# Output biases by the first turn's scatter, gate weights in two early slots, and the embedding gate's first steps by row block

## The chip, the cores and the metric

The kernel runs on one core of one Trainium2 chip, as one program with one launch. The metric is the device time of an execution in microseconds (us); less is better. PE is the matrix engine (TensorE), DVE the vector engine, ACT the scalar engine, POOL the GpSimd engine; SP only issues DMAs and waits. PSUM has eight banks of 128 partitions by 512 f32 words.

## The reference

Everything is f32, for 256 tokens of width 1024. A first block (pooling, attention, a mixture of experts, a gated embedding, a norm) is followed by two layers of another kind. What matters here is the end of the first block:

```
x = x + moe(rmsnorm(x, g_ffn), w_router, b_router, w_gate_up, b_gate_up, w_down, b_down)
gate = sigmoid(rmsnorm(x, g_ple) @ w_ple_gate)          # 1024 x 1024
x = x + (p @ w_ple_proj) * gate                         # p has 256 columns
x = rmsnorm(x, g_final)
```

In `moe` each token picks 4 of 32 experts; for a picked expert `e` with gate value `gate_e` it adds `gate_e * (act(h @ w_gate_up[e] + b_gate_up[e]) @ w_down[e] + b_down[e])`. So the output biases contribute, for each token, the sum over its experts of `gate_e * b_down[e]`. After the first block come two layers that begin with a feed-forward part: `x + 0.5 * swiglu(rmsnorm(x, ffa_norm), w_in, w_out)`.

## The kernel before

**Order.** Each engine has one hand-written list of instructions; engines wait for one another on semaphores only. Four pieces follow one another in each list: `first_part` (pooling and attention), `experts_part`, the gated embedding (the functions whose names begin with `ple_`), and two calls of the layer functions. SP's list sets the order of nearly all DMAs, on one queue.

**Experts.** The expert weights are 192 units of 2 MB (six to an expert), streamed through eight slots: `ring[0]` to `ring[5]`, and two in scratch (slots 6 and 7). The loop has one turn an expert for 64 tokens; `experts_part` first computes how many turns there are (`turns_ready`, here 32), and every engine loads that number into registers (`turns_of`) before its loop. In a turn PE multiplies the selected tokens `xsel` by units 0 to 3 (`product`, L2221), turns the result, gathers the next turn's tokens with a 0/1 matrix `sel` (`gather_turn`), turns `gsel` (the selection times the gates; `selT`), and multiplies by units 4 and 5 into the bank that ACT copies to `y`. The next turn's `scatter` (L2229, 4 matmuls with 64 rows each) adds `gselT` times `y` to four accumulators `acc(t, v)`: t is the block of 128 tokens, v the half of 512 columns. SP issues a unit's successor when PE has read it (L2135). Before turn 0 `y` and `gselT` are zero, so the first scatter adds nothing.

**Output biases.** They sit in scratch (`M_BDOWN`). After the loop PE turns `gate` (L2278), ACT copies it (L2323), PE adds the biases by 4 matmuls with only 32 rows (L2284), and then does the last scatter. The gate and up biases `b_gu` are loaded four times over, because the turn's number indexes them.

**Gated embedding.** SP loads `w_ple_proj` and the turned p into `ring[0]` after the last group's third turn (`ple_proj_sync`), and the two halves of `w_ple_gate` into scratch after the last unit is read (`ple_weights_sync`). PE: for each (t, v) two matmuls of p (`proj`, L2530) and four transposes of x (L2536); then four groups of eight matmuls (L2551), `pgate(v, t)`. DVE first sums all four accumulators into x (L2678), then scales the turned x (L2683). ACT: four squares, two roots, and then, in `ple_act`, `splits.to(SPLIT_SLOTS - 1)`, the casts of four pieces of the first layer's weights, and only then the first sigmoid:

```python
    splits.to(SPLIT_SLOTS - 1)
    for v in range(2):
        ple_sigmoid_act(k, act, 0, v)
        ple_squares_act(k, act, 0, v)
```

From there ACT and DVE alternate: sigmoid (L2566), product and sum (L2626 to L2628), squares (L2575, L2577), the variance (L2638 to L2647), a root, h (L2656); first for t = 0, v = 0 and 1, then for t = 1. PE turns h for the first layer (L750), between the two blocks it has 20 matmuls whose result nobody reads (`spare_pe`, L731), and then the feed-forward product starts (L831, L832).

**Layer weights.** SP sends the layers' weights in 0.5 MB pieces into four `raw` buffers (L2801). These lie over `ring[0]`, where the operands of `proj` are, so SP first waits:

```python
        k.enter("ple")
        k.filled(sp, ("proj", 1, 1))
        for layer in range(LAYERS):
```

ACT casts a piece to `w_hi` (L612), POOL computes the rest `w_lo` (L618).

Of the kernel before, what the change touches and what calls it, by code (L numbers as in the profile page):

```python
# [13 lines left out]
P = 128  # L14
# [263 lines left out]
def bc(ap, shape):  # L278
    return ap.to_broadcast(shape)
# [1482 lines left out]
def first_part(k, dram, block):  # L1762
# [11 lines left out]
    def _(sp):  # L1774
# [29 lines left out]

        sp.wait_ge(*k.at("rev_ready", 1))
# [209 lines left out]
SL = 64  # L2015
# [3 lines left out]
M_BGU, M_BDOWN, M_ROUTE = 5508, 7556, 8580  # L2019
# [42 lines left out]
def moe_uses(start):  # L2062
# [9 lines left out]
    uses.add(("gateT",), 0)  # L2072
# [6 lines left out]
def experts_part(k, dram, block):  # L2079
# [10 lines left out]
    def turn_filled(eng, key, it):  # L2090
        eng.wait_ge(full_of[key], it + (2 if key[0] == "gather" else 1))
        return k.bank[TURN_KEYS[key]], free_of[key]
# [6 lines left out]
    rank, gate, bgu = k.s(M_RANK, NT, TURNS), k.s(M_GATE, NT, TURNS), k.s(M_BGU, ROUNDS * E, 16)  # L2099
    b_down = k.s(M_BDOWN, D)  # L2100
# [4 lines left out]
    count, gateT, more = small(552, 1), small(560, NT, P), small(556, ROUNDS)  # L2105
# [12 lines left out]
    def _(sp):  # L2118
# [26 lines left out]
        sp.wait_ge(full_of["y",], last * GROUP + GROUP)  # L2145
        with k.inside("ple"):
            ple_weights_sync(k, sp, dram)
            ple_small_sync(k, sp, dram)

    @block.tensor  # L2150
    def _(pe):
# [11 lines left out]
        def gather(b, half, *rows_of):  # L2163

            for t in rows_of:
                for j in range(4):
                    c = 4 * half + j
                    last = nc.tensor.matmul(b[:, j * P:(j + 1) * P], k.h[:, t, c * P:(c + 1) * P], sel[:, t, :],
                                            start=(t + j == 0), stop=(t == 1 and j == 3))
            return last  # L2170
# [29 lines left out]
        k.evacuated(pe, ("count",), ("rank", 1))  # L2200
        turns, groups_n = turns_of(pe)
# [23 lines left out]
        def scatter(last=False):  # L2225
            for t in range(NT):
# [13 lines left out]
        with pe.Fori(0, groups_n) as group:  # L2240
            for turn in range(GROUP):
# [9 lines left out]
                scatter()  # L2251
# [13 lines left out]
                for t in range(NT):  # L2265
                    last = nc.tensor.transpose(b[:, t * P:(t + 1) * P], gsel[:, t, :], k.c("ident"))
                last.then_inc(full, 1)
# [5 lines left out]
        for half in range(2):  # L2273
            turn_evacuated(pe, ("gather", half), turns)
# [4 lines left out]
        last.then_inc(full, 1)  # L2279
        k.evacuated(pe, ("gateT",))  # L2280
        pe.wait_ge(*k.at("b_loaded", 16 * (ROUNDS + 1)))
        for t in range(NT):
            for v in range(2):
                nc.tensor.matmul(k.bank[4 + 2 * t + v][:, :], gateT[0:E, t, :], b_down[0:E, v * 512:(v + 1) * 512], start=False, stop=False)  # L2284
        for key in (("selT",), ("y",)):
            turn_evacuated(pe, key, turns)
        scatter(last=True)
        with k.inside("ple"):
            ple_first_pe(k, pe)

    @block.scalar
    def _(act):
# [14 lines left out]
        nc.scalar.activation(ex, ex, ACT.Exp).then_inc(k.sem("exp_ready"), 1)  # L2307
        turns, groups_n = turns_of(act)
# [13 lines left out]
        b, free = k.filled(act, ("gateT",))  # L2322
        nc.scalar.copy(gateT[0:E], part(b, NT, P)[0:E]).then_inc(free, 1)  # L2323

    @block.vector
    def _(dve):
# [57 lines left out]
        V_.memset(y, 0.0).then_inc(free_of["y",], 1)  # L2384
        V_.memset(gselT, 0.0).then_inc(free_of["selT",], 1)
        dve.wait_ge(free_of["y",], 1)
# [994 lines left out]
```

## Time and profile before

| what | value |
|---|---|
| median of 3 runs | 2469.76 us (2467.59 to 2471.13) |
| span of the profiled execution (first to last instruction) | 2465.0 us |
| the profiled execution's own time | not printed apart from its span; the runs are 2.6 to 6.1 us above the span |
| PE busy in the span | 2426.4 us (98%) |
| DVE, ACT, POOL busy | 924.0, 887.1, 1010.1 us |
| DMA in the expert loop | 430 GB/s |
| expert loop on PE | 119.95 us to about 1033.6 us |
| gated embedding on PE, up to the first product of layer 0 | about 1033.6 us to 1088.91 us |

Times in the rows are us from the span's start. A row of a chain of waits gives start, length, and what the end waited on. A row of a timeline gives start, length, engine, line, operation, tiles, shapes and count, with the idle time before it in brackets. A f32 matmul has two records.

### The profile page before, as it was taken

The page shows a single profiled execution, that of the slowest core. Times are in us where ns is not written, and L with a number is a line of the kernel's source. Part 1 is how long each engine was busy: PE and PEld are TensorE (multiplying, and loading weights), DVE is VectorE, ACT ScalarE, POOL GpSimd, SP SyncE. Part 2 cuts the span into 40 slices and gives each one's busy share as a digit, 9 for nine tenths or more (in the row PEclk, how much of TensorE's full clock was granted, in tenths as well). Part 3 has the DMA queues.
Part 4 walks back from the last instruction along what each step waited for, and adds up shares of the span by engine and source line. Part 5 has one row for each costly group of instructions (what it writes and reads, how often), then busy time and mean ns, then how long its engine had stood idle before and what let it go on. Part 6 is the DMA issues. An engine that isn't in the chain of part 4 may idle for free.

```text
span 2465.0 us, 34958 instructions
## 1 busy us (share of the span) xinstructions
PE 2426.4 (98%) x13879; PEld 1715.0 (70%) x13879; DVE 924.0 (37%) x1746; ACT 887.1 (36%) x1455; POOL 1010.1 (41%) x428
## 2 busy tenths in 40 slices
PE   8999999999999999999999999999999999999999
PEld 6744444444444444468889899888888898998887
DVE  5622222222222222253238764332432378653322
ACT  6411111111111111154457634544444477425443
POOL 0000000000000000038878445788788795546986
PEclk9999999999999999999999999999999999999999
DMA  7799999999999999935555333465555553324554
GB/s 285 292 399 428 430 430 429 430 429 430 430 429 430 429 430 430 381 120 199 189 168 178 105 103 129 155 209 189 177 189 193 169 175 120 120 95 154 200 185 144
DMA packets 96703, 653.66 MB, mean 265 GB/s; under 512 B 10880, under 2 KB 13232, under 8 KB 69968
## 3 DMA queue, kind: packets, MB, share of 16 engines
q1 hardware_dynamic: 96592, 652.11, 68.1%
q8 instruction: 78, 1.28, 0.2%
q14 instruction: 33, 0.27, 0.0%
HBM read 651.01 MB, written 1.06 MB: 265 GB/s over the span
## 4 chain that ended last, share of the span: by engine, by line
PE 87%; DMA 9%; DVE 1%; ACT 1%; issue 1%; POOL 0%; SPq 0%; DVEq 0%; ACTq 0%
PE bank L2221 20%; PE bank L831 13%; PE bank L631 10%; PE bank L633 10%; PE bank L632 10%; PE bank L832 7%; DMA ring<-in_expert_units 5%; DMA scratch<-in_expert_units 4%; PE bank L2208 4%; PE bank L1226 3%; PE bank L2229 2%; PE bank L2551 1%; PE bank L2237 1%; PE bank L1104 1%; PE bank L1075 1%
## 5 line engine op out<-in xcount | busy, mean ns | idle before, releaser
L618 POOL TENSOR_TENSOR w_lo<-raw,w_hi 128x1024 fp32r<-128x1024 f32 (+2 forms) x424 | 1009.9, 2410 | 1442.5 <-ACT w_hi L612 1442.5
L2221 PE MATMUL bank<-ring,scratch 128*64 128x512 f32 x2304 | 514.1, 596 | 12.8 <-DMA ring<-in_expert_units 11.7
L831 PE MATMUL bank<-hT_both,w_hi 128*128 128x512 f32 x1408 | 496.2, 398 | 1.7 <-DVE hT_both L722 1.7
L612 ACT CAST w_hi<-raw 128x1024 fp32r<-128x1024 f32 (+2 forms) x424 | 421.1, 1042 | 166.6 <-PE bank L633 159.2
L832 PE MATMUL bank<-hT_both,w_lo 128*128 128x256 f32 x1408 | 394.8, 280 | 0.0
L2221 PEld LDWEIGHTS bank<-ring,scratch 128*64 128x64 f32 x2304 | 160.5, 137 | 327.6 <-issue 321.7
L831 PEld LDWEIGHTS bank<-hT_both,w_hi 128*128 128x128 f32 x1408 | 264.7, 188 | 67.0 <-issue 3.0
L2461 DVE TENSOR_TENSOR scratch<-bank,scratch 128x512 f32<-128x512 f32 x64 | 44.3, 692 | 597.3 <-PE bank L2237 593.2
L832 PEld LDWEIGHTS bank<-hT_both,w_lo 128*128 128x128 f32 x1408 | 265.9, 189 | 0.6
L909 DVE TENSOR_REDUCE scratch<-bank 128x256 f32<-128x512 f32 x88 | 60.9, 692 | 356.6 <-PE bank L832 356.6
L2221 PE MATMUL bank<-scratch 128*64 128x512 f32 x768 | 172.1, 596 | 3.1 <-DMA scratch<-in_expert_units 3.1
L631 PE MATMUL bank<-hT_both,w_hi 128*128 128x256 f32 x576 | 165.6, 287 | 0.0
L633 PE MATMUL bank<-hT_both,w_lo 128*128 128x256 f32 x576 | 163.2, 283 | 0.0
L632 PE MATMUL bank<-hT_both,w_hi 128*128 128x256 f32 x576 | 163.1, 283 | 0.0
L631 PE MATMUL bank<-w_hi,act_hi 128*128 128x512 f32 (+1 forms) x376 | 145.9, 388 | 0.0
L632 PE MATMUL bank<-w_lo,act_hi 128*128 128x512 f32 (+1 forms) x376 | 145.8, 388 | 0.0
L633 PE MATMUL bank<-w_hi,act_lo 128*128 128x512 f32 (+1 forms) x376 | 145.7, 388 | 0.0
L2316 ACT ACTIVATE scratch<-scratch 128x256 f32<-128x256 f32 x64 | 26.7, 417 | 307.7 <-DVE scratch L2464 307.7
L2208 PEld LDWEIGHTS bank<-scratch,h_rows 128*128 128x128 f32 x1024 | 119.3, 192 | 26.0 <-issue 26.0
L2314 ACT COPY scratch<-bank 128x512 f32<-128x512 f32 x64 | 37.5, 585 | 269.3 <-PE bank L2221 269.3
L2221 PEld LDWEIGHTS bank<-scratch 128*64 128x64 f32 x768 | 53.5, 137 | 108.0 <-issue 106.9
L2208 PE MATMUL bank<-scratch,h_rows 128*128 128x128 f32 x1024 | 128.1, 278 | 0.0
(380 smaller groups left out, 3371.9 us busy)
## 6 DMA issues: line engine op xcount, KB each, us to landing
ring<-in_expert_units SPq DMA_DIRECT2D x144, 2048.0 KB, 29.6
raw<-in_layer_halves SPq DMA_DIRECT2D x408, 512.0 KB, 3.9
scratch<-in_expert_units SPq DMA_DIRECT2D x48, 2048.0 KB, 30.5
ring<-in_first_units SPq DMA_DIRECT2D x11, 1024.0 KB, 10.4
scratch<-in_ple_units SPq DMA_DIRECT2D x2, 2048.0 KB, 11.0
raw<-in_layer_halves SPq DMA_DIRECT2D x8, 424.0 KB, 3.2
scratch<-in_norm_gains SPq DMA_DIRECT2D x6, 512.0 KB, 5.8
raw<-in_layer_halves SPq DMA_DIRECT2D x4, 384.0 KB, 3.2
```

The lines of the kernel that those rows point to most:

```text
L612: k.nc.scalar.copy(k.w[0][i % SPLIT_SLOTS][:, at], k.raw[n % RAW_SLOTS][:, 0:at.stop - at.start]).then_inc(k.shared("weights_hi"), 1)
L618: k.nc.gpsimd.tensor_tensor(k.w[1][i % SPLIT_SLOTS][:, at], k.raw[n % RAW_SLOTS][:, 0:at.stop - at.start], k.w[0][i % SPLIT_SLOTS][:, at], ...
L631: nc.tensor.matmul(out, lhsT[0], rhs[0], start=start, stop=False)
L632: nc.tensor.matmul(out, lhsT[0], rhs[1], start=False, stop=False)
L633: return nc.tensor.matmul(out, lhsT[1], rhs[0], start=False, stop=stop)
L831: nc.tensor.matmul(bank[:, :], w[0], both, start=start, stop=False)
L832: return nc.tensor.matmul(bank[:, 0:S], w[1], both[:, 0:S], start=False, stop=stop)
L909: return k.nc.vector.tensor_reduce(out, b[:, :].rearrange("p (part n) -> p n part", part=2), AX.X, ALU.add)
L1226: last = nc.tensor.matmul(b[:, h * P:(h + 1) * P], lhsT[:, h, :], rhs[:, h, :], start=True, stop=True)
L2208: last = nc.tensor.matmul(b[:, j * P:(j + 1) * P], k.h[:, t, c * P:(c + 1) * P], sel[:, t, :], start=(t == 0), stop=(t == 1))
L2221: last = nc.tensor.matmul(b[g * SL:(g + 1) * SL, :], lhsT[:, c, :], w[:, c, g, :], start=start and c == 0, stop=stop and c == 3)
L2229: ins = nc.tensor.matmul(k.bank[b][:, :], gselT[half, t, :], y[half, :], start=False, stop=last)
```

## The change

The output biases are loaded near the kernel's start into rows 0 to 31 (columns 0 to 511) and 64 to 95 (columns 512 to 1023) of `y`, which DVE has zeroed. Before the loop DVE writes the gates of all experts into `gsel` in the same two places, PE turns them, ACT copies them to `gselT`, and turn 0's scatter, which used to add zeros, adds the biases. The block behind the loop (turn, copy, 4 matmuls) is gone. `b_gu` is loaded once, indexed by the turn's number modulo 32. The gate's denominators are computed before the count of turns instead of after the first `take`.

The halves of `w_ple_gate` go to `ring[4]` and `ring[5]`, each as soon as the last expert has read that slot. PE's list behind the loop is now: proj(0,0), last scatter, proj(0,1), transposes of t = 0, proj(1,0), gate products (0, v = 0), transposes of t = 1, gate products (0, v = 1), proj(1,1), and the two gate products of t = 1. In this sentence proj(t, v) has the block first. DVE sums and scales one block, then the other.

```diff
@@ first_part, SP, behind load(7)
+        sp.wait_ge(*k.at("zeros_ready", 1))
+        with k.inside("moe"):
+            moe_down_biases_sync(k, sp, dram)
         sp.wait_ge(*k.at("rev_ready", 1))
@@ first_part, DVE
+        nc.vector.memset(k.s(M_Y, 512), 0.0)
         link(nc.vector.memset(k.hT[:, 0:2, :], 0.0))
@@
 def moe_biases_sync(k, sp, dram):
-    bgu, b_down = k.s(M_BGU, ROUNDS * E, 16), k.s(M_BDOWN, D)
-    for r in range(ROUNDS):
-        sp.dma_start(bgu[:, r * E:(r + 1) * E, :], dram["b_gu"]).then_inc(k.sem("b_loaded"), 16)
-    sp.dma_start(b_down[0:E, :], dram["b_down"].rearrange("o e d -> (o e) d")).then_inc(k.sem("b_loaded"), 16)
+    sp.dma_start(k.s(M_BGU, E, 16), dram["b_gu"]).then_inc(k.sem("b_loaded"), 16)
+
+def moe_down_biases_sync(k, sp, dram):
+    y, b_down = k.s(M_Y, 512), dram["b_down"].rearrange("o e d -> (o e) d")
+    for v in range(2):
+        sp.dma_start(y[v * SL:v * SL + E, :], b_down[:, columns_half(v)]).then_inc(k.sem("b_loaded"), 16)
@@ experts_part, SP
-        sp.wait_ge(full_of["y",], last * GROUP + GROUP)
+        sp.wait_ge(k.sem("first_unit_read"), last * (GROUP * EXPERT_UNITS // 2) + (GROUP - 1) * EXPERT_UNITS // 2 + 2)
         with k.inside("ple"):
-            ple_weights_sync(k, sp, dram)
+            ple_weights_sync(k, sp, dram, 0)
+        sp.wait_ge(full_of["rows", 1], last * GROUP + GROUP)
+        with k.inside("ple"):
+            ple_weights_sync(k, sp, dram, 1)
             ple_small_sync(k, sp, dram)
@@ experts_part, PE, ahead of the loop
         k.evacuated(pe, ("count",), ("rank", 1))
+        pe.wait_ge(*k.at("gate_ready", 1))
+        selection_turned(k.bank[TURN_KEYS["selT",]]).then_inc(full_of["selT",], 1)
         turns, groups_n = turns_of(pe)
@@ experts_part, PE, behind the loop
-        b, full = k.claim(pe, ("gateT",))
-        pe.wait_ge(*k.at("gate_ready", 1))
         for t in range(NT):
-            last = nc.tensor.transpose(b[0:E, t * P:(t + 1) * P], gate[:, t, 0:E], k.c("ident"))
-        last.then_inc(full, 1)
-        k.evacuated(pe, ("gateT",))
-        pe.wait_ge(*k.at("b_loaded", 16 * (ROUNDS + 1)))
-        for t in range(NT):
-            for v in range(2):
-                nc.tensor.matmul(k.bank[4 + 2 * t + v][:, :], gateT[0:E, t, :], b_down[0:E, v * 512:(v + 1) * 512], start=False, stop=False)
-        for key in (("selT",), ("y",)):
-            turn_evacuated(pe, key, turns)
-        scatter(last=True)
+            scatter((t,), last=True)
         with k.inside("ple"):
-            ple_first_pe(k, pe)
+            ple_proj_pe(k, pe, 0, 1)
+            ple_turned_pe(k, pe, 0)
+            ple_proj_pe(k, pe, 1, 0)
...
@@ experts_part, DVE, between sel_ready and the count of turns
+        dve.wait_ge(*k.at("exp_ready", 1))
+        link(V_.tensor_tensor(ex, ex, chosen, ALU.mult))
+        link(V_.tensor_reduce(den, ex, AX.X, ALU.add))
+        link(V_.reciprocal(den, den))
+        for t in range(NT):
+            ins = V_.tensor_scalar(gsel[:, t, :].rearrange("p (v n) -> p v n", v=2)[:, :, 0:E], bc(ex[:, t, :].unsqueeze(1), [P, 2, E]),
+                                   den[:, t:t + 1], None, ALU.mult)
+        ins.then_inc(k.sem("gate_ready"), 1)
+
         b, free = k.filled(dve, ("count",))
@@ layers_part, PE
-        ple_gate_pe(k, pe)
+        ple_gate_pe(k, pe, 0, 0)
+        ple_turned_pe(k, pe, 1)
+        ple_gate_pe(k, pe, 0, 1)
+        ple_proj_pe(k, pe, 1, 1)
+        ple_gate_pe(k, pe, 1, 0)
+        ple_gate_pe(k, pe, 1, 1)
```

Nothing in `ple_act`, in SP's wait for `proj(1,1)`, or in the layers is changed.

## Rows read from the trace of the kernel before

**Rows 1.** Page, part 4: the chain that ended last, share by engine.

```profile
PE 87%; DMA 9%; DVE 1%; ACT 1%; issue 1%; POOL 0%; SPq 0%; DVEq 0%; ACTq 0%
```

**Rows 2.** The chain from 1015 to 1130 us: start, length, what.

```profile
1026.64 7.04 PE bank L2221 x32
...
1034.59 5.45 PE bank L2284 x8
1040.04 3.51 PE bank L2229 x8
...
1045.46 0.44 PE bank L2536 x4
1045.90 1.72 PE bank L2530 x4
...
1052.37 27.48 PE bank L2551 x64
```

**Rows 3.** The chain of the whole span: turn 0's scatter.

```profile
127.04 1.92 PE bank L2229 x8
```

**Rows 4.** Stretches of 1 us: length, busy PE, PEld, DVE, ACT, POOL, clock, DMA, GB/s.

```profile
1036.00:1037.00 1.00, 1.00 (x3) 0.51 (x2) 0.00 (x0) 0.00 (x0) 0.00 (x0) 0.70 0.81 344
...
1043.00:1044.00 1.00, 1.00 (x3) 0.30 (x2) 0.78 (x2) 1.00 (x4) 0.00 (x0) 0.89 1.07 459
```

**Rows 5.** Timeline from the layer weights' first DMA to the first sigmoid.

```profile
1051.96 67.61 SPq L2801 DMA_DIRECT2D raw<-in_layer_halves  x18
...
1055.91 1.05 ACT L612 CAST w_hi<-raw 128x1024 fp32r<-128x1024 f32 x1 [1.69 <-DMA raw<-in_layer_halves]
...
1060.33 1.04 ACT L612 CAST w_hi<-raw 128x1024 fp32r<-128x1024 f32 x1 [0.21 <-DMA raw<-in_layer_halves]
...
1062.69 0.69 ACT L2566 ACTIVATE scratch<-bank,scratch 128x512 f32<-128x512 f32 x1
```

**Rows 6.** Timelines of DVE, ACT and PE, from h to the feed-forward product.

```profile
1072.71 1.41 DVE L2656 SCALAR_TENSOR_TENSOR h_rows<-bank,scratch 128x512 f32<-128x512 f32 x2 [0.49 <-ACT scratch L2585]
...
1085.89 1.41 DVE L2656 SCALAR_TENSOR_TENSOR h_rows<-bank,scratch 128x512 f32<-128x512 f32 x2 [0.27 <-ACT scratch L2585]
...
1079.94 0.69 ACT L2566 ACTIVATE scratch<-bank,scratch 128x512 f32<-128x512 f32 x1 [1.10 <-PE bank L2551]
...
1080.47 4.81 PE L731 MATMUL bank<-w_hi 128*128 128x512 f32 x20
...
1088.91 0.47 PE L831 MATMUL bank<-hT_both,w_hi 128*128 128x512 f32 x1 [0.90 <-DVE hT_both L722]
```

**Rows 7.** Timeline ahead of the expert loop: end of the count, gates, first product.

```profile
117.80 0.14 DVE L2429 CAST scratch<-scratch 128x1 int32<-128x1 f32 x1
...
119.26 0.22 DVE L2438 TENSOR_TENSOR scratch<-scratch 128x64 f32<-128x64 f32 x1
...
119.95 7.09 PE L2221 MATMUL bank<-ring,scratch 128*64 128x512 f32 x32 [1.07 <-issue]
119.96 0.63 DVE L2442 TENSOR_TENSOR scratch<-scratch 128x64 f32<-128x64 f32 x4
```

**Rows 8.** Stretches in the expert loop, columns as in rows 4.

```profile
124.00:125.00 1.00, 1.00 (x8) 0.31 (x5) 0.00 (x0) 0.00 (x0) 0.00 (x0) 1.00 0.04 16
...
145.00:146.00 1.00, 1.00 (x8) 0.41 (x6) 0.00 (x0) 0.00 (x0) 0.00 (x0) 1.00 0.31 131
...
300.00:600.00 300.00, 300.00 (x1574) 129.50 (x1574) 68.37 (x176) 39.69 (x71) 0.00 (x0) 1.00 1.01 430
```

**Rows 9.** Timeline of the kernel's first microseconds.

```profile
0.92 0.48 DVE L1973 MEMSET hT<- 128x512 f32 x1 [0.92 <-PEq L3377]
...
1.92 3.78 PE L512 MATMUL bank<-first_lo 128*128 128x512 f32 x8 [1.92 <-DVE first_lo L1974]
```

**Rows 10.** SP's timeline, then the page's DMA issues: KB, median us to landing.

```profile
1004.42 0.34 SPq L2504 DMA_DIRECT2D ring<-in_ple_units  x1
...
ring<-in_ple_units SPq DMA_DIRECT2D x1, 1024.0 KB, 26.3
```

More of the change, by code:

```diff
@@ L2104, in experts_part @@
     den = small(550, NT)
[L2105 removed]
+    count, more = small(552, 1), small(556, ROUNDS)
     turns_i, groups_i, groups = small(553, 1).bitcast(I32), small(554, 1).bitcast(I32), small(555, 1)
@@ L2223, in product, with scatter @@
             return last
-        def scatter(last=False):
-            for t in range(NT):
+        def scatter(rows_of, last=False):
+            for t in rows_of:
                 for v in range(2):
@@ L2264, in _ @@
                 b, full = turn_claim(pe, ("selT",), it)
-                for t in range(NT):
-                    last = nc.tensor.transpose(b[:, t * P:(t + 1) * P], gsel[:, t, :], k.c("ident"))
-                last.then_inc(full, 1)
+                selection_turned(b).then_inc(full, 1)
                 b, full = turn_claim(pe, ("y",), it)
@@ L2307, in _ @@
         nc.scalar.activation(ex, ex, ACT.Exp).then_inc(k.sem("exp_ready"), 1)
+        act.wait_ge(full_of["selT",], 1)
+        nc.scalar.copy(gselT, part(k.bank[TURN_KEYS["selT",]], NT, P)).then_inc(free_of["selT",], 1)
         turns, groups_n = turns_of(act)
@@ L2395, in _ @@
         h_of(0)
+        dve.wait_ge(*k.at("b_loaded", 3 * 16))
+        V_.memset(gsel, 0.0).then_inc(free_of["y",], 1)
         hT_of(1, 0)
@@ L2540, in ple_gate_pe @@
-def ple_gate_pe(k, pe):
-    hT = k.s(PLE_HT, KC, S)
-    for t in range(NT):
-        for v in range(2):
-            if t == 0:
-                pe.wait_ge(*k.at(f"ple_arrived{v}", 16))
-            w = k.s(PLE_W[v], KC, 512)
-            k.evacuated(pe, ("norm", 0, t, 0), ("norm", 0, t, 1))
-            b, full = k.claim(pe, ("pgate", v, t))
-            for c in range(KC):
-                last = k.nc.tensor.matmul(b[:, :], hT[:, c, t * P:(t + 1) * P], w[:, c, :], start=(c == 0), stop=(c == KC - 1))
-            last.then_inc(full, 1)
+    b, full = k.claim(pe, ("proj", v, t))
@@ new lines, in ple_proj_pe, with ple_turned_pe, ple_gate_pe @@
+    for c in range(2):
+        last = k.nc.tensor.matmul(b[:, :], pT[:, c, t * P:(t + 1) * P], w[:, c, v * 512:(v + 1) * 512], start=(c == 0), stop=(c == 1))
+    last.then_inc(full, 1)
+def ple_turned_pe(k, pe, t):
+    for v in range(2):
+        b, full = k.claim(pe, ("norm", 0, t, v))
+        for j in range(4):
+            c = 4 * v + j
+            last = k.nc.tensor.transpose(b[:, j * P:(j + 1) * P], k.x[:, t, c * P:(c + 1) * P], k.c("ident"))
+        last.then_inc(full, 1)
+def ple_gate_pe(k, pe, t, v):
+    hT, w = k.s(PLE_HT, KC, S), ple_gate_weights(k, v).rearrange("p (c n) -> p c n", n=512)
+    if t == 0:
+        pe.wait_ge(*k.at(f"ple_arrived{v}", 16))
+    for c in range(KC):
+        if c % 4 == 0:
+            k.evacuated(pe, ("norm", 0, t, c // 4))
+            if c == 0:
+                b, full = k.claim(pe, ("pgate", v, t))
+        last = k.nc.tensor.matmul(b[:, :], hT[:, c, t * P:(t + 1) * P], w[:, c, :], start=(c == 0), stop=(c == KC - 1))
+    last.then_inc(full, 1)
```

71 lines of the change are left out of this document (26 added, 45 removed).

## The prediction, made before the changed kernel was run

> **What bounds the kernel now.** I read the page's chain first, then the chain of waits by stretch, then the timelines at the three places the change touches. PE carries 87% of the chain that ended last [rows 1], so time is won only where PE's list gets shorter and nothing else ends later. There are three regimes. Inside the expert loop PE is at first the slower one; DMA runs dry twice, at 124 us and again at 145 us, because a unit's successor can only be sent when PE has read its slot, and from then on it moves 430 GB/s without a pause to the end of the loop [rows 8]. So the loop ends a fixed time after PE begins it, and bytes taken out before it are worth nothing: all eight slots are full when DMA stops at 124. Behind the loop, PE is busy from 1033.68 us (1026.64 + 7.04) through the bias products, the scatter, the p products and the 64 gate records to about 1079.85 [rows 2]. The reader should then see how thin PE's lead is: ACT's last sigmoid waited only 1.10 us for PE [rows 6]. Just behind PE runs a second chain: SP sends layer weights at 1051.96, when the last proj product is done; ACT casts four pieces (first at 1055.91, the fourth ends 1060.33 + 1.04 = 1061.37), loads its table, and starts the first sigmoid at 1062.69 [rows 5]. From there ACT and DVE alternate without a pause that PE causes, up to that 1.10 us.
>
> **PE's list behind the loop.** Before: 1033.68 to 1079.85 is 46.2 us. Removed: the turn, ACT's copy and the four 32-row matmuls, from 1033.68 to 1040.04, 6.4 us [rows 2]. The scatter took 3.51 us there and 1.92 in the loop [rows 2, 3], the same eight records. The granted clock explains it: it left full speed (2.4 GHz) at about 1036.3 us (mean 0.70 in 1036 to 1037) and came back at about 1043.1 (0.89 in 1043 to 1044) [rows 4], and what PE did before was the pause for ACT's copy and then the 32-row matmuls. Without them I expect full speed, so 1.92. New list: 4 proj groups at 1.72, 4 transpose groups at 0.44, the scatter at 1.92, 64 gate records at 27.48 / 64 = 0.43: 6.88 + 1.76 + 1.92 + 27.48 = 38.0 us [rows 2, 3]. PE saves 8.1 us. What hides the waits: proj(0,0) (1.72) covers ACT's copy of y, a single copy of one bank, shorter than that; scatter(1) and proj(0,1) (2.7 us) cover DVE's two sums of block 0, and proj(1,0) with the second transposes its two scalings. Each of these four handles one bank of 512 columns, about half of L2656's 1.41 us for two [rows 6]; without that cover each would show once, 0.7 us. The sums of block 1 have the 6.9 us of the first gate group.
>
> **The weights.** proj's operands are issued at 1004.42 and land 26.3 us later, 1030.7 [rows 10], 3 us ahead of their use now at 1033.7. `w_ple_gate` is sent some 11 to 15 us earlier than before, behind those on the same queue. At 430 GB/s [rows 8] a half takes 4.9 us, so they land at about 1036 and 1041; PE wants them at about 1042 and 1050. No expert unit waits behind them. Worth 0; before, they were no wait either.
>
> **Where the stall goes.** SP's wait for proj(1,1) is untouched, since `raw` lies over `ring[0]`. But proj(1,1) now comes behind two groups of gate products. Between the end of the loop and it PE has 4 x 1.72 + 1.92 + 4 x 0.44 + 32 records x 0.43 (13.74) = 24.3 us; before it was 1051.96 - 1033.68 = 18.3 [rows 2, 3, 5]. The first layer piece leaves 6.0 us later, relative to the end of the loop. Queued behind it: the landing (3.95 us to the first cast), four casts on ACT, which stand ahead of the first sigmoid in ACT's list, and the table load; 10.73 us from the DMA to the sigmoid, as before [rows 5]. DVE waits for the sigmoids, and PE for DVE's h. So the whole ACT and DVE chain moves 6.0 us later, though the first gate bank was full 10 us before. It gets back only the 1.10 us that the last sigmoid had waited for PE [rows 6]. Net on the path: 6.0 - 1.1 = +4.9 us where PE alone would say -8.1. DVE's and ACT's own work is the same, and the layer behind is PE's, so nothing later takes it back. POOL's four pieces also end 6 us later, before `spare_pe` needs them.
>
> **Before the loop.** Turn 0's scatter does what it did, with other numbers. On DVE five instructions now stand ahead of the count of turns. Three of them took 119.26 to 119.96, 0.70 us; two writes of `gsel` at 0.63 / 4 = 0.16 each make 1.0 us [rows 7]. The count ended at 117.80 + 0.14, and PE's first product came 2.0 us later, with 1.07 us of pause that nothing explains but the loading of registers; PE's gathers were done before. So the loop starts up to 1.0 us late. Below: if PE's pause hangs on its gathers alone, 0.4 us, for two more transposes (a group of four is 0.44 [rows 2]). I take 1.0, because DVE shows the same two microseconds between the end of its gates, 120.59, and its first loop work. What stood there for 0.6 to 0.7 us leaves a place where DVE is not late. The new memset of `y` stands ahead of everything on DVE. The memset of `hT` took 0.48 us, and PE's first matmul waited for its cast until 1.92 [rows 9]; its warming matmuls run until x is turned. So +0.5, between 0 (if x had not arrived) and 0.5. The two new bias loads are issued while SP would wait for the distance table: 0, and if that cover were gone, two issues at 0.34 us [rows 10]. The saved loads of `b_gu`: 0, by the idle DMA at 124 us [rows 8]. `it & 31` costs DVE a register step in a loop where it idles: 0. The front together: +1.5.
>
> **The clock.** PE is done at 1033.7 + 1.5 + 38.0 = 1073.2, and h of block 0 comes at 1072.71 + 7.5 = 1080.2 [rows 6]: 7 us or more in which PE has nothing. `spare_pe` (4.81 us) follows, and then PE waits again, from about 1086 to h of block 1 at 1085.89 + 6.4 = 1092.3 [rows 6]. Before, no pause was near this long, and the one fall of the clock lasted 6.8 us [rows 4]. What falls before spare work costs nothing. What is still low when the feed-forward product begins costs half of its time: between 0 and 3.4 us (half of 6.8). I take the middle, +1.7, as neither row is near.
>
> Against this stands a rule of the Trainium skill, page "TensorE: Matmul & The Clock Gate", section "Why this matters for your kernels": pauses between bursts of matmuls put the clock back to its lower level. By it both pauses end at 1.2 GHz. That is rival 1.
>
> **Sum.** -1.1 + 6.0 + 1.5 + 1.7 = +8.1 us. The profiled execution's span would go from 2465.0 to 2473.1. The median of the runs is 4.8 us above the span before, and I carry the difference: 2469.8 + 8.1 = 2477.9. The feed-forward product L831 begins at 1088.91 + 6.4 = 1095.3.
>
> **Rivals.**
> 1. The clock's fall in full: low for 6.8 us from the start of the feed-forward product. 4.9 + 1.5 + 3.4 = +9.8, 2479.6. For it: two pauses of 6 to 8 us, where a short one and narrow matmuls were enough. Against: `spare_pe` between them.
> 2. Clock and front are both free: only the late weights, +4.9, 2474.7. For it: PE paused 1.07 us ahead of the loop already [rows 7], so a part of a delay there may be absorbed. Against: the register loads on DVE and PE follow the count.
> 3. The other side, faster: the place is ACT's list between the fourth cast and the first sigmoid. If the pieces don't hold the sigmoids, because they land and are cast while PE works on the second gate group, PE's end decides: -8.1 + 1.5 = -6.6, 2463.2. It decides if the fourth cast ends no later than before plus 1.1 us relative to the sigmoid chain, that is if the piece leaves no more than 1.1 us later. Against: SP's wait is on proj(1,1), two gate groups down PE's list, and ACT works in order. The rows leave little room.
>
> **Chances.** Forecast 0.60, rival 1 0.17, rival 2 0.15, rival 3 0.08. What a measurement of this kernel can tell from no change is 0.2%, 4.9 us: below 2464.8 faster, above 2474.7 slower. Rival 2 sits on that border, so half of it, and a little of the forecast's lower end, is "same": 0.09. Slower 0.83, faster 0.08. Range 2472.5 to 2483: the chain term alone less a miscount of a group, up to rival 1 with the runs' own spread (1.8 us) on top. It leaves out rival 3 and a tail.
>
> **What the profile after would show.** Behind the loop no L2278, L2284, L2323, the last scatter at 1.9 us and the clock at 1.00 through it; proj(1,1) and SP's first raw piece at about 1059.5; the first sigmoid at about 1070.2, right behind the fourth cast; PE idle from about 1073 to 1081 and again before 1092; L831 first at about 1095.3, and the clock there below 1.00. The first expert product at about 121.5. The prediction is wrong if the first sigmoid comes before 1064, if the raw pieces leave before proj(1,1), or if PE has work up to h of block 0.

## The result, and the profile after

The changed kernel takes 2479.36 us (median of 4 runs, 2477.68 to 2482.16), the kernel before 2468.68 (4 runs, 2464.10 to 2471.13): ratio 1.0047, 95% interval 1.0035 to 1.0058, so slower by 11.6 us (the two medians differ by 10.7). The forecast was 2477.9 and slower. The profiled execution took 2479.33 us with a span of 2477.5 us, 12.5 more than the span before. Lines moved down by 14 to 18: L2229 is L2246, L2530 L2544, L2536 L2554, L2551 L2568, L2566 L2583, L2656 L2673, L2801 L2817. L612, L731, L750 and L831 are unchanged.

PE's list behind the loop is what the forecast made of it: 38.4 us from the end of the loop to the end of the gate groups, where 38.0 was forecast. The chain of waits of the changed kernel from 1015 to 1130 us (start, length, what), which answers to [rows 2]:

```profile
1035.14 1.91 PE bank L2544 x4
1037.05 1.92 PE bank L2246 x8
1038.97 1.91 PE bank L2544 x4
1040.88 0.87 PE bank L2554 x8
1041.76 1.72 PE bank L2544 x4
1043.47 6.87 PE bank L2568 x16
1050.34 0.87 PE bank L2554 x8
1051.21 6.87 PE bank L2568 x16
1058.08 1.73 PE bank L2544 x4
...
1061.15 7.10 DMA raw<-in_layer_halves
...
1070.63 0.69 ACT scratch L2583
```

The bias products and the turning of `gate` are gone, and the scatter takes 1.92 us where it took 3.51. But the chain leaves PE at 1059.81, the end of p product (1,1). From there it is a DMA, ACT and DVE. PE's own third and fourth gate groups don't stand in it. The timelines of SP and ACT, for [rows 5]:

```profile
1059.83 12.47 SPq L2817 DMA_DIRECT2D raw<-in_layer_halves  x7
```

```profile
1063.84 1.05 ACT L612 CAST w_hi<-raw 128x1024 fp32r<-128x1024 f32 x1 [10.61 <-DMA raw<-in_layer_halves]
...
1068.28 1.04 ACT L612 CAST w_hi<-raw 128x1024 fp32r<-128x1024 f32 x1 [0.20 <-DMA raw<-in_layer_halves]
...
1070.63 0.69 ACT L2583 ACTIVATE scratch<-bank,scratch 128x512 f32<-128x512 f32 x1
...
1081.94 0.69 ACT L2583 ACTIVATE scratch<-bank,scratch 128x512 f32<-128x512 f32 x1
```

ACT sat idle for 10.61 us before its first cast, although the first gate bank was full at 1050.34. The last two sigmoids wait for no PE now, where the last one waited 1.10 us [rows 6]. What PE has left is two pauses. Its timeline from 1080 us on:

```profile
1081.46 1.97 PE L750 MATMUL bank<-const,h_rows 128*128 128x128 f32 x8 [7.93 <-DVE h_rows L2673]
1083.08 5.58 PE L731 MATMUL bank<-w_hi 128*128 128x512 f32 x20
1093.43 1.97 PE L750 MATMUL bank<-const,h_rows 128*128 128x128 f32 x8 [4.76 <-DVE h_rows L2673]
1096.10 0.77 PE L831 MATMUL bank<-hT_both,w_hi 128*128 128x512 f32 x1 [0.71 <-DVE hT_both L722]
```

The clock stands in the seventh place after the time in the stretches (columns as in rows 4). It stayed full through the scatter, and was at its lower level, 1.2 GHz, from 1077.9 to 1084.7 and from 1091.6 to 1101.8, 5.7 us of that inside the feed-forward product:

```profile
1036.00:1037.00 1.00, 1.00 (x5) 0.21 (x3) 0.00 (x0) 0.00 (x0) 0.00 (x0) 1.00 1.00 426
...
1092.00:1094.00 2.00, 0.57 (x3) 0.58 (x4) 1.69 (x4) 0.20 (x1) 0.00 (x0) 0.50 0.00 0
1096.00:1097.00 1.00, 0.90 (x3) 0.83 (x4) 0.88 (x2) 1.00 (x3) 0.00 (x0) 0.50 0.00 0
1101.00:1102.00 1.00, 1.00 (x5) 0.81 (x5) 1.00 (x4) 0.00 (x0) 0.78 (x1) 0.60 1.01 360
```

The front, for [rows 7, 9]. Two memsets now stand ahead of the cast, and the gates (from 117.27) ahead of the count:

```profile
0.92 0.48 DVE L1976 MEMSET scratch<- 128x512 f32 x1 [0.92 <-PEq L3398]
...
2.46 0.79 PE L512 MATMUL bank<-first_lo 128*128 128x512 f32 x1 [2.46 <-DVE first_lo L1978]
```

```profile
117.27 0.22 DVE L2428 TENSOR_TENSOR scratch<-scratch 128x64 f32<-128x64 f32 x1
...
119.42 0.14 DVE L2448 CAST scratch<-scratch 128x1 int32<-128x1 f32 x1
...
121.41 1.94 PE L2238 MATMUL bank<-ring,scratch 128*64 128x512 f32 x8 [1.73 <-issue]
```

The same instructions of both traces, set side by side, give the shift of after against before: 0.54 us at PE's first product, 1.46 at the first expert product, 1.46 at the end of the loop, 7.87 at the first raw piece, 7.94 at the first sigmoid, 6.73 at the transposes of block 1, 7.19 at L831, 9.75 at 1108 us (times of such a comparison are those of the first profile of before). Behind that it is still 9.8 at 1550 us, grows in two steps to 11.4 at 1850, and is 12.5 at the end of the span.

### The profile page after: what moved, and what is told of

It is laid out like the page before. It is cut to its first block, busy times and chain, and to the rows that moved or that the text cites. A ratio compares the mean times of both kernels' runs of the same rounds, so it can differ in the third digit from the quotient of the medians.

```text
span 2477.5 us, 34979 instructions
## 1 busy us (share of the span) xinstructions
PE 2426.1 (98%) x13871; PEld 1717.1 (69%) x13871; DVE 922.9 (37%) x1748; ACT 888.0 (36%) x1455; POOL 1009.6 (41%) x428
## 3 DMA queue, kind: packets, MB, share of 16 engines
q8 instruction: 78, 1.28, 0.2%
## 4 chain that ended last, share of the span: by engine, by line
PE 86%; DMA 10%; DVE 2%; ACT 1%; issue 1%; POOL 0%; SPq 0%; DVEq 0%; ACTq 0%
PE bank L2238 20%; PE bank L831 13%; PE bank L631 10%; PE bank L632 10%; PE bank L633 10%; PE bank L832 7%; DMA ring<-in_expert_units 5%; DMA scratch<-in_expert_units 4%; PE bank L2225 4%; PE bank L1226 3%; PE bank L2246 2%; PE bank L2254 1%; PE bank L1104 1%; PE bank L1075 1%; PE bank L2568 1%
## 5 line engine op out<-in xcount | busy, mean ns | idle before, releaser
L831 PE MATMUL bank<-hT_both,w_hi 128*128 128x512 f32 x1408 | 500.2, 400 | 1.5 <-DVE hT_both L722 1.5
L612 ACT CAST w_hi<-raw 128x1024 fp32r<-128x1024 f32 (+2 forms) x424 | 421.9, 1042 | 179.7 <-PE bank L633 157.9
L832 PE MATMUL bank<-hT_both,w_lo 128*128 128x256 f32 x1408 | 396.4, 282 | 0.0
L831 PEld LDWEIGHTS bank<-hT_both,w_hi 128*128 128x128 f32 x1408 | 265.7, 189 | 68.5 <-issue 3.2
L832 PEld LDWEIGHTS bank<-hT_both,w_lo 128*128 128x128 f32 x1408 | 267.2, 190 | 0.6
```

Of the source, the lines that this page charges most:

```text
L612: k.nc.scalar.copy(k.w[0][i % SPLIT_SLOTS][:, at], k.raw[n % RAW_SLOTS][:, 0:at.stop - at.start]).then_inc(k.shared("weights_hi"), 1)
L831: nc.tensor.matmul(bank[:, :], w[0], both, start=start, stop=False)
L832: return nc.tensor.matmul(bank[:, 0:S], w[1], both[:, 0:S], start=False, stop=stop)
```

## The experiments

My theory is the forecast's: p product (1,1) comes late, SP holds the raw pieces for it, and ACT's four casts of them stand ahead of every sigmoid. What else could make the same time is PE's own order, the clock, the front, and the weights or biases in their new places. Each verdict is read against the kernel before, run on the same chip. The medians of two kernels that did not run together compare less well: where a sentence below subtracts such medians, the ratios in the table say how much of it is safe.

| kernel | median us (runs) | before, same chip | ratio, 95% interval |
|---|---|---|---|
| changed kernel | 2479.36 (4) | 2468.68 | 1.0047 [1.0035, 1.0058] |
| e1_proj_early | 2466.89 (11) | 2468.11 | 0.9996 [0.9987, 1.0005] |
| e2_casts_behind | 2464.47 (11) | 2468.11 | 0.9984 [0.9975, 0.9993] |
| e4_clock_kept | 2483.99 (5) | 2468.11 | 1.0064 [1.0050, 1.0077] |
| e7_early_front | 2465.87 (11) | 2468.11 | 0.9991 [0.9982, 1.0000] |
| e5_blocks_undone | 2463.97 (11) | 2467.97 | 0.9984 [0.9975, 0.9992] |
| e6_late_weights | 2466.15 (11) | 2467.97 | 0.9995 [0.9987, 1.0004] |
| e8_casts_between | 2462.85 (12) | 2467.97 | 0.9987 [0.9978, 0.9995] |
| e9_clock_second | 2476.22 (5) | 2467.97 | 1.0033 [1.0020, 1.0046] |
| e3_front | 2476.27 (6) | 2467.39 | 1.0043 [1.0030, 1.0056] |
| e10_undone_front | 2461.84 (10) | 2467.39 | 0.9976 [0.9967, 0.9985] |
| e11_before_again | 2473.06 (1) | 2467.39 | one run |

**e1_proj_early.** One call moved in PE's list.

```diff
+        ple_proj_pe(k, pe, 1, 1)
         ple_gate_pe(k, pe, 0, 0)
         ple_turned_pe(k, pe, 1)
         ple_gate_pe(k, pe, 0, 1)
-        ple_proj_pe(k, pe, 1, 1)
         ple_gate_pe(k, pe, 1, 0)
```

> The changed kernel with one line of PE's list moved: proj(1,1) stands ahead of the first gate group instead of behind the second. Theory (the layer weights leave late, and ACT's casts of them hold the sigmoids): the first raw piece leaves at about 1045.2 us instead of 1059.8, the first sigmoid starts at about 1058.8 instead of 1070.6 (now it waits for the roots and four casts), PE has no pause before h of block 0, the clock stays up, and the first L831 comes at about 1083.9 instead of 1096.1. Span about 2462.4 (2477.5 - 12.2 - 3 for the clock), so some 6 us under the kernel before. Rival (the new order by blocks, or the work ahead of the loop, is what costs, and the weights only happen to leave later): first L831 stays at 1094 or later and the span at 2474 or more. Rival (only the clock's fall in the pauses costs): about 2474.

All of the loss is gone, by moving two matmuls (four records); the kernel takes the same time as before within the noise. SP sends the first piece at 1045.48 us, and ACT's timeline no longer shows a wait for a DMA. The pieces lie ready when the roots are done. SP's line and ACT's:

```profile
1045.48 1.85 SPq L2817 DMA_DIRECT2D raw<-in_layer_halves  x4
```

```profile
1055.12 3.87 ACT L612 CAST w_hi<-raw 128x1024 fp32r<-128x1024 f32 x4
...
1060.30 0.69 ACT L2583 ACTIVATE scratch<-bank,scratch 128x512 f32<-128x512 f32 x1
```

The casts themselves now hold the sigmoid for their 3.87 us. L831 begins at 1085.77, 3.1 us ahead of before. Here the expectation missed: it had 1083.9 with the clock up. PE idled 3.87 us before block 1's transposes, the clock was at its lower level from 1082.0 to 1088.8, and by 1099 the lead was 1.76 us. The span, 2465.2, is 2.8 above the one expected.

**e2_casts_behind.** The other end of the same wait: PE keeps the changed order, ACT casts after block 0's root.

```diff
-    splits.to(SPLIT_SLOTS - 1)
     for v in range(2):
         ple_sigmoid_act(k, act, 0, v)
         ple_squares_act(k, act, 0, v)
     with k.inside(0):
         ple_root_act(k, act, 0)
+    splits.to(SPLIT_SLOTS - 1)
```

> The changed kernel with PE's list as it is, and one line of ACT's list moved: the casts of the first four layer pieces stand behind block 0's root instead of ahead of the first sigmoid. Theory: the raw pieces still leave at about 1059.8, but the first sigmoid starts at about 1054.5 and the sigmoid of block 1 follows the casts at about 1070.6; PE has no pause before h of block 0; first L831 at about 1083.8, span about 2462.3. If what matters is when the pieces leave, and not ACT's order (a rival: the layer itself waits for its weights), L831 stays near 1094 to 1096 although the sigmoids come early.

This separates PE's order from the casts. The raw pieces leave as late as in the changed kernel (1063.13, in an execution that was 4.8 us late against before at the first expert product, where the changed kernel's was 1.46; its clock was low from 11.9 to 15.3 and again from 18.8 to 22.2 us), and 14.9 us of time are gone all the same. Less the 3.3 us between these two, the first sigmoid (1057.85) and L831 (1087.23) are within 0.2 us of what was expected. PE's order by row block costs next to nothing by itself; it costs through what ACT does in order. ACT's timeline:

```profile
1057.85 0.69 ACT L2583 ACTIVATE scratch<-bank,scratch 128x512 f32<-128x512 f32 x1
...
1067.75 1.98 ACT L612 CAST w_hi<-raw 128x1024 fp32r<-128x1024 f32 x2
```

**e4_clock_kept.** Spare matmuls in both pauses: 28 ahead of block 0's transposes, 44 behind.

```diff
+    if k.part == 0:
+        spare_pe(k, pe, 28)
     lnorm_pe(k, pe, 0, 0)
     if k.part == 0:
-        spare_pe(k, pe)
+        spare_pe(k, pe, 44)
```

> The changed kernel with more matmuls whose result nobody reads in PE's two pauses: 28 ahead of the transposes of h of block 0, 44 instead of 20 behind them. They keep PE busy and wait for nothing on the path. Theory: the granted clock stays at 1.00 at the start of the feed-forward product, the first L831 comes at about 1095.7 (1096.1 less the slow transposes), the product's first 6 us lose nothing, and the span is about 3 us less, 2474.5. Rival (the clock is not what costs between 1096 and 1108; the late layer weights are): the clock stays up and the span doesn't change, 2477. Rival (the clock is the whole loss): about 2465.

It misfired as a repair. The spare work borrows a bank that ACT's third sigmoid frees, so it could not start in the pause. PE's timeline:

```profile
1082.04 9.49 PE L731 MATMUL bank<-w_hi 128*128 128x512 f32 x28 [8.78 <-ACT scratch L2583]
...
1092.16 10.25 PE L731 MATMUL bank<-w_hi 128*128 128x512 f32 x44
...
1104.41 0.47 PE L831 MATMUL bank<-hT_both,w_hi 128*128 128x512 f32 x1 [1.12 <-DVE hT_both L722]
```

The fillers pushed L831 8.3 us later than in the changed kernel, and the time grew by only 4.6 (medians of kernels that did not run together): from L831 on the clock was full, and the shift against before did not grow (15.5 us there, 15.6 at 1500 us). The span is 7.3 us above the expected 2474.5, so this run says what a full clock does behind L831 and nothing about a repair.

**e9_clock_second.** The repair of that test: only the second pause is filled.

```diff
-    for j in range(20):
+    for j in range(40):
...
-                           start=(j == 0), stop=(j == 19))
+                           start=(j == 0), stop=(j == 39))
```

> The changed kernel with 40 spare matmuls instead of 20 between the two row blocks' transposes, so that TensorE works from 1083.1 to about 1093.3, where it was idle from 1088.7 to 1093.4. The first fall of the clock (1077.9 to 1084.7) stays. Theory (the second fall costs the transposes and the first feed-forward product about 3 us): clock at 1.00 from about 1085 on, the four last transposes take 0.7 instead of 1.13 us, the first feed-forward product starts at 1095.0 to 1095.8 instead of 1096.1, the shift against the kernel before stays at about 6.5 through 1108 instead of growing to 9.75, time 2475 to 2477. Rival (the extra shift behind the first product has another cause, weights arriving late for one): time 2479 to 2480 although the clock stays up.

PE worked until 0.46 us before the transposes, which took 1.32 us together instead of 1.97. PE's timeline and a stretch:

```profile
1084.72 9.88 PE L731 MATMUL bank<-w_hi 128*128 128x512 f32 x40
1095.06 1.32 PE L750 MATMUL bank<-const,h_rows 128*128 128x128 f32 x8 [0.46 <-DVE h_rows L2673]
1097.28 0.47 PE L831 MATMUL bank<-hT_both,w_hi 128*128 128x512 f32 x1 [0.90 <-DVE hT_both L722]
```

```profile
1096.00:1098.00 2.00, 1.10 (x8) 0.80 (x7) 1.56 (x3) 1.93 (x4) 0.00 (x0) 1.00 0.00 0
```

The start times are 1.7 us above what was expected, because this execution was already 3.12 us late at the first expert product, where the changed kernel's was 1.46. From there to 1096 us it lost 5.1 us against before (3.12 to 8.24), where the changed kernel lost 8.3 (1.46 to 9.74). The median is 3.1 us lower. Both say that the second fall costs about 3 us.

**e7_early_front** and **e3_front.** One edit on the front, on e1 and on the changed kernel: the new memset behind the cast, the gates and their transposes behind the count.

```diff
-        nc.vector.memset(k.s(M_Y, 512), 0.0)
         link(nc.vector.memset(k.hT[:, 0:2, :], 0.0))
...
+        nc.vector.memset(k.s(M_Y, 512), 0.0).then_inc(k.sem("y_cleared"), 1)
...
-        pe.wait_ge(*k.at("gate_ready", 1))
-        selection_turned(k.bank[TURN_KEYS["selT",]]).then_inc(full_of["selT",], 1)
         turns, groups_n = turns_of(pe)
+        pe.wait_ge(*k.at("gate_ready", 1))
+        selection_turned(k.bank[TURN_KEYS["selT",]]).then_inc(full_of["selT",], 1)
```

> proj(1,1) early as in the first of these, and the work ahead of the loop moved too: the new memset stands behind the cast that PE's first matmul waits for, the gates and their writes stand behind the count of turns on DVE, and PE turns them after it has loaded its registers. Theory: PE's first matmul starts 0.54 us earlier, the first expert product at about 120.2 instead of 121.4, and all behind moves with it: 1.2 us less than with proj(1,1) early alone, span about 2461.2. Rival (the loop ends when DMA has moved its bytes, and where PE begins it is worth nothing): the loop's end doesn't move, and the span is that of the kernel with proj(1,1) early.

> The changed kernel with its front put back in order: the first memset stands behind the cast of zeros, and the gates (VectorE) and their transposes (TensorE) stand behind the count of the turns. Theory (0.5 us for the memset ahead of the first product and 1.0 us for the gates ahead of the count, both carried to the end): first product at 1.9 instead of 2.46, first expert product at 120.0 to 120.4 instead of 121.4 where the clock at the start is the same, time 1.0 to 1.8 us below the changed kernel's 2479.4: 2477.6 to 2478.4. Rival (the loop takes the late start back while it waits for weights): the loop ends where it did, time 2479 to 2480.

In e7 the first expert product comes at 120.11 us, 1.62 ahead of e1, and the end of the loop and L831 both come 1.28 ahead (L831 at 1084.49): the loop does not take the start back. Its span, 2463.4, is 2.2 above the one expected, as e1's was 2.8 above its own.

In e3 PE's first product stands at 1.92 us again and the first expert product at 119.73, 1.68 earlier than in the changed kernel. All of that arrives at block 1's transposes, at 5.05 us of shift instead of 6.73. The line of its PE timeline:

```profile
119.73 1.51 PE L2238 MATMUL bank<-ring,scratch 128*64 128x512 f32 x6
```

By medians the repair gives 1.0 us in e7, 2.1 in e10 (below) and 3.1 in e3. The last two compare kernels that did not run together, and against before the ratios of e3 and the changed kernel differ by 0.0004, 1 us. e3's median, 2476.27, lies 1.3 us below the range expected for it. Its trace shows one reason: the second fall of the clock lasted 6.8 us (1090.4 to 1097.3) where the changed kernel's lasted 10.2, which is some 1.3 of the 3.1 us between the two traces at 1096. A stretch of e3 and then of the changed kernel:

```profile
1098.00:1100.00 2.00, 2.00 (x14) 1.75 (x13) 2.00 (x1) 0.00 (x0) 2.00 (x1) 1.00 0.54 160
```

```profile
1098.00:1100.00 2.00, 2.00 (x8) 1.71 (x7) 2.00 (x4) 1.21 (x1) 2.00 (x2) 0.50 0.00 0
```

So the front is worth 1 to 2 us.

**e5_blocks_undone.** The part with the block order undone, everything else of the change kept.

```diff
+        scatter(range(NT), last=True)
+        with k.inside("ple"):
+            for t in range(NT):
+                for v in range(2):
+                    ple_proj_pe(k, pe, t, v)
+                    ple_turned_pe(k, pe, t, (v,))
...
+        for t in range(NT):
+            for v in range(2):
+                ple_gate_pe(k, pe, t, v)
```

> The changed kernel with one part undone: TensorE issues the p products, the transposes of x and the gate groups in the order of the kernel before (all four scatters, then p product and transpose by half, then four gate groups), and VectorE makes all four x sums first. The biases in the first scatter, the weights in slots 4 and 5 and the new front stay. Theory (the row-block order lets go of the raw pieces late, and that is what the time went to): the loop still ends at about 1035.1, the raw pieces go out at about 1045.7 instead of 1059.8, the first sigmoid starts at 1058 to 1061, the first feed-forward product at 1083 to 1086, and the time is 2466 to 2470. Rival (the biases or the weights in ring slots cost it): the time stays at 2476 to 2481.

4.0 us faster than before, 15.4 below the changed kernel. So the order by row block, with ACT's list as it is, costs 15 us, and the rest of the change is a gain. Some 3 us of that (2466.89 against 2463.97) stay when only p product (1,1) is moved, as in e1: there ACT's last root stands at 1055.01, here at 1049.88 although this execution reached the loop 1.5 us later, and the sigmoids follow. The time is 2 us below the range expected. The end of the loop (1036.64) and the first raw piece (1047.82) came 1.5 and 2.1 us later than expected, as this execution was 3.3 us late at the first expert product instead of 1.5 (the clock had fallen once more in its first 15 us); the first sigmoid and L831 fell into their ranges. PE's and ACT's timelines:

```profile
1048.06 27.63 PE L2567 MATMUL bank<-ring,scratch 128*128 128x512 f32 x64
...
1076.32 4.81 PE L731 MATMUL bank<-w_hi 128*128 128x512 f32 x20
1082.55 1.31 PE L750 MATMUL bank<-const,h_rows 128*128 128x128 f32 x8 [1.42 <-DVE h_rows L2672]
1084.77 0.47 PE L831 MATMUL bank<-hT_both,w_hi 128*128 128x512 f32 x1 [0.90 <-DVE hT_both L722]
```

```profile
1051.83 1.04 ACT L612 CAST w_hi<-raw 128x1024 fp32r<-128x1024 f32 x1 [1.75 <-DMA raw<-in_layer_halves]
...
1058.68 0.69 ACT L2582 ACTIVATE scratch<-bank,scratch 128x512 f32<-128x512 f32 x1
```

**e6_late_weights.** As e5, with the gate weights sent after the last unit is read.

```diff
-        sp.wait_ge(k.sem("first_unit_read"), last * (GROUP * EXPERT_UNITS // 2) + (GROUP - 1) * EXPERT_UNITS // 2 + 2)
+        sp.wait_ge(full_of["y",], last * GROUP + GROUP)
         with k.inside("ple"):
             ple_weights_sync(k, sp, dram, 0)
-        sp.wait_ge(full_of["rows", 1], last * GROUP + GROUP)
-        with k.inside("ple"):
             ple_weights_sync(k, sp, dram, 1)
```

> As the run with the block order undone, and the gate weights are sent only when the last unit has been read (about 1035), into the same slots 4 and 5. Theory (early weights buy nothing while the first gate group starts at about 1046): they land at 1043 to 1047, the first gate group starts 0 to 1 us later than with early weights, and the time is within 1.5 us of that run. Rival (early weights are what keeps TensorE fed): the gate groups start 4 us or more later and the time grows by 4 us.

Neither theory as written. PE's gate groups start in their place (1048.42, no wait), and yet the time is 2.2 us above e5's. The price stands on ACT: the raw pieces, sent 0.35 us later than in e5, queue behind the weights and the small loads. The first sigmoid comes 3.0 us after e5's, PE pauses 2.98 us before block 1's transposes instead of 1.42, and in this execution the clock is low from 1083.7 to 1090.5, which it never is there in e5. So by the traces the 2.2 us are the late pieces and a fall of the clock together. ACT's timeline and a stretch, whose last two columns say that the DMA engines were busy all of it, at 383 GB/s:

```profile
1055.57 1.04 ACT L612 CAST w_hi<-raw 128x1024 fp32r<-128x1024 f32 x1 [5.13 <-DMA raw<-in_layer_halves]
```

```profile
1050.00:1054.00 4.00, 4.00 (x11) 1.71 (x9) 0.78 (x3) 0.20 (x1) 0.00 (x0) 1.00 1.01 383
```

**e8_casts_between.** e7, and the four casts go two by two into ACT's waits for DVE.

```diff
-    splits.to(SPLIT_SLOTS - 1)
     for v in range(2):
         ple_sigmoid_act(k, act, 0, v)
+        splits.to(SPLIT_SLOTS - 2 + v)
         ple_squares_act(k, act, 0, v)
```

> The version with p product (1,1) ahead of the first gate group and with the gates behind the count (2465.9), and ScalarE's four casts of raw pieces, 3.87 us that stood ahead of the first sigmoid at 1059.0, go two by two into its waits between sigmoid and squares of row block 0 (2.33 us each). Theory (ScalarE's list in front of the sigmoids sets the end, not TensorE's gate groups): first sigmoid at about 1055, root of row block 0 at about 1065, first feed-forward product at 1080.5 to 1082 instead of 1084.5, TensorE's pause before the last transposes 1 to 2 us instead of 3.9, so that the clock may stay at 1.00; time 2460 to 2463. Rival (the gate groups, which end at 1072.5, or GpSimd's low halves set the end): first product at 1084 to 1085, time 2465 to 2467.

As expected, but for the clock, which may have stayed up and did not. ACT's timeline shows two casts taking 1.98 us of a wait of 2.3, with 0.45 left:

```profile
1055.00 0.69 ACT L2583 ACTIVATE scratch<-bank,scratch 128x512 f32<-128x512 f32 x1
1055.59 1.98 ACT L612 CAST w_hi<-raw 128x1024 fp32r<-128x1024 f32 x2
1058.01 0.60 ACT L2592 ACTIVATE scratch<-bank 128x512 f32<-128x512 f32 x1 [0.45 <-DVE h_rows L2645]
```

L831 begins at 1081.65, 2.8 us ahead of e7's 1084.49. The clock still fell, from 1081.1 to 1084.5, after a pause of 1.72 us. The times don't separate the two kernels clearly: the medians differ by 3.0 us, but they did not run together, and the ratios against before differ by 0.0004, 1 us.

**e10_undone_front.** e5 with the front of e3.

> The version with the block order undone (2463.97) and the same repair of the front: what is left of the change is the biases in the first scatter and the weights in slots 4 and 5. Theory: 1.0 to 1.8 us below that version, 2462.2 to 2463.0, and below the kernel before by 5 to 6 us. Rival (its front costs nothing there): 2463.5 to 2464.5.

2461.84 us, the lowest median of this study, 0.4 us below the range expected: 5.6 us, 0.24% below before (0.15 to 0.33%). The intervals of e2, e5 and e8 overlap this one. What it keeps is the biases in the first scatter and the early weights. In its profiled execution L831 began at 1081.82, 7.1 us ahead of before, and the clock never fell after 5.8 us.

**e11_before_again.** The kernel before, profiled once more.

> The kernel before, profiled a second time. The changed kernel's profiled execution is 12.5 us longer in span than the one of before, but the medians differ by 9.6 to 11.6 us, and some 2.8 us of the 12.5 appear little by little in the two layers. Theory (the first profiled execution of before was one of its short ones, 2465.0 us against a median of 2468 to 2470): this one has a span of 2465.5 to 2469, and the shift against the first creeps up by 1 to 3 us behind the first feed-forward product as well. Rival (the changed kernel loses 2.8 us in the layers): no such creep, span 2464.5 to 2465.5.

Its span was 2471.2, longer than expected. The shift against the first profile is 1.9 us at the first expert product, 2.7 at the end of the loop, 1.0 at block 1's transposes and at L831, 3.8 at 1096 us and 6.2 at the end. So 2.4 us appear behind 1096 in the same kernel. The step of 2.8 before that is the clock, low from 1089.3 to 1096.1. So is the gain of 1.7 between the loop and the transposes: behind the loop the clock was low for 3.4 us here (1041.5 to 1044.9) and for 6.8 in the first profile, and the bias matmuls took 3.7 us instead of 5.45. Stretches of the second and then of the first profile of before:

```profile
1088.00:1090.00 2.00, 1.09 (x9) 0.65 (x7) 1.22 (x3) 1.50 (x3) 0.00 (x0) 0.82 0.00 0
1090.00:1092.00 2.00, 2.00 (x6) 1.71 (x7) 2.00 (x4) 1.98 (x3) 1.31 (x1) 0.50 0.03 8
```

```profile
1090.00:1092.00 2.00, 2.00 (x13) 1.76 (x12) 2.00 (x4) 1.81 (x2) 2.00 (x1) 1.00 0.04 8
```

## Why the prediction was right, and which terms were off

| term | predicted | measured | from |
|---|---|---|---|
| front | +1.5 | +1.46 | 0.54 at the first product, 0.92 more at the first expert product |
| late raw pieces | +6.0 | +6.4 | 7.87 - 1.46 |
| wait for PE given back | -1.1 | -1.2 | 7.94 at the first sigmoid, 6.73 at block 1's transposes |
| clock | +1.7 | +3.0 | 0.46 in the transposes, 2.56 from L831 to 1108 us |
| sum | +8.1 | +9.75 | shift at 1108 us (the rows above give 9.66) |
| layers | 0 | +2.8 | shift at the end 12.5 |

**The chain.** The mechanism held at each link: proj(1,1), SP, landing, casts, sigmoids. e1 cuts the first link and e2 the one between the casts and the sigmoids; each alone removes the whole loss (e1 the same as before, e2 0.16% below it). The gap of 0.4 us is a count made with 1.72 for each p product, where two of the four took 1.91.

**PE's list.** PE's gate groups ended at 1079.85 before and at 1073.53 after (1081.46 - 7.93): 6.3 us earlier, where 8.1 - 1.5 = 6.6 was forecast. Where the block order and with it the wait for raw pieces is undone and the front repaired (e10), L831 comes 7.1 us earlier and the time is 5.6 lower. That is the forecast's rival 3, which had -6.6 with the front still late. Its mechanism is real; its condition, that the pieces leave no more than 1.1 us later, was missed by 5.3 us. The gain was turned into a pause of PE. Some of the 8.1 us is the execution's: the list that the change removes and shortens took 46.2 us in the first profile of before and 44.5 in e11, as the clock was low for less of it.

**Front.** Right in both parts, and e3 confirms it. The loop passed the delay on undiminished (1.46 at its start and at its end), so rival 2, which had the front free, falls.

**Clock.** This is the mis-sized term. I took the middle of 0 and 3.4; the second fall cost 3.0, since it lasted 10.2 us, not 6.8, and 5.7 of these fell into the feed-forward product. In e3's execution, with two pauses much like them (7.60 and 4.49 us), it lasted 6.8 and cost about 1.6 (0.46 in the transposes, 1.17 from L831 to 1096), which is the forecast's figure; so the size of this term was not in the kernel alone. Rival 1's time, 2479.6, is nearer to the result than the forecast's, and what I held against it, `spare_pe` between the pauses, did not help: the spare work ended 4.8 us before block 1's h. The rule of the Trainium skill (page "TensorE: Matmul & The Clock Gate", section "Why this matters for your kernels") holds: both pauses ended at 1.2 GHz. e9 prices the second at about 3 us by filling it. But the reference was off too. The profile of before that I worked from shows no fall there, and e11 shows one that costs 2.8 us for the same code and the same pause (1.40 us). So the kernel before pays this in some of its executions, and the change's share of the clock, in the median, probably lies below 3.0; how often before pays was not measured.

**Layers.** The forecast had nothing there. Of the 2.8 us, 1.6 are two steps, at 1580 to 1650 and 1780 to 1850 us. They are a matter of the execution: e11 has both and a third at 2280 to 2350 (2.4 together) in the kernel before, and e3, with the changed kernel's layers, has none. The other 1.2 stand behind VectorE's last instruction, where the span goes on for 2.4 us in both profiles of before, 2.9 in e3 and six others, and 3.6 in the changed kernel, e2, e5 and e7; at most 0.5 of that is common to all the changed kernels. e11 also says what the 4.8 us were that I carried from span to median. Of them 1.8 are time outside the span (2479.33 - 2477.5, and 2473.06 - 2471.2 in e11). The other 3.0 made up for a short profiled execution. So it is partly luck that 2477.9 is only 1.5 us off: the span that was forecast, 2473.1, is 4.4 us short of the measured 2477.5, and 3.0 came back through the carried difference. Where the steps come from was not tried.

**Weights.** "Worth 0" holds for this kernel, where the pieces leave at 1059.8, long after the weights have landed. In e5's order it is worth 2.2 us (e5 and e6 ran together), not by PE but by the pieces behind them on the queue; the forecast had looked only at who reads the weights.

## What to carry to other kernels

Before an instruction is moved down one engine's list, look up who waits for its semaphore beyond the data it makes: here two matmuls that take 1.7 us together freed a buffer, and the DMA into it stood ahead of ACT's whole remaining list. A shorter list on the busiest engine shows in the time only if nothing in order on a second engine is made to wait for its later items; where the second engine has a wait of fixed length anyway (2.3 us here), put the work that nobody needs yet into it. And profile the kernel before twice: on one chip its executions ran from 2463.16 to 2472.43 us, nearly as far apart as the change is from it, and 2.8 us of the 6.2 between its two profiles are one fall of the clock.

## What was not expected of the hardware

The same pause gave two clocks. In two executions of the kernel before, with 1.42 and 1.40 us idle ahead of the last transposes, the clock stayed at 1.00 in the first and was at 0.50 from 1089.3 to 1096.1 in the second; e5 and e10 kept it after 1.42 us, e8 lost it for 3.4 us after 1.72 and e2 for 3.4 after 1.96. And the start varies: in five of the thirteen profiles (e2, e5, e6, e9, e11) the clock fell to 0.50 once more, from about 10.7 to 14.1 us or from 11.9 to 15.3. At 60 us this put them 1.7 to 1.9 us behind the changed kernel (e11 behind the first profile of before), and e2, where it fell twice, 3.3.

A whole product can run at two paces at full granted clock. The steps in the layers are not pauses: from 1583 to 1634 us every pair of L831 and L832 is a little slower, until the product is 0.7 us longer, in the changed kernel, e1, e8, e9, e10 and e11, and in e2 to e7 it is not. In the first feed-forward product the kernel before (both times), the changed kernel, e1, e4 and e10 run at one pace, and the others gain 0.6 us on them between 1100 and 1134 us. What decides the pace was not tried. A shift between two traces therefore carries 0.7 to 0.9 us for each such product that no edit here explains.
